# Block 1's up projection from its fifth group on: one product moves the high and low parts of x, and the convolution opens from their sum

## What is computed

```python
h = rmsnorm(x, ffn_norm_g[layer])
up = causal_dwconv(h @ ffn_w_up[layer], ffn_conv_w[layer], ffn_conv_b[layer])   # 1024 -> 5632, then 3 taps along the tokens
gate, val = jnp.split(up, 2, axis=-1)                                            # 2816 each
x = x + (jax.nn.silu(gate) * val) @ ffn_w_down[layer]
```

## Time and profile before

| | us |
|---|---|
| median of 3 runs (lowest, highest) | 1839.29 (1838.99, 1840.1) |
| the profiled execution | 1838.47 |
| its span, first to last instruction | 1836.7 |
| TensorE busy | 1822.3 |
| VectorE busy | 1336.1 |
| ScalarE busy | 1023.9 |

### The profile page before, as it was taken

How to read it: one execution, slowest core, us unless ns; L and a number is a source line. 1 busy time by engine, 2 the same in 40 slices (tenths; PEclk the granted TensorE clock), 3 DMA queues, 4 the chain that set the end, 5 groups by cost and what they waited for, 6 DMA issues and landing times.

```text
span 1836.7 us, 26700 instructions
## 1 busy us (share of the span) xinstructions
PE 1822.3 (99%) x10726; PEld 1601.4 (87%) x10726; DVE 1336.1 (73%) x1898; ACT 1023.9 (56%) x1216; POOL 6.6 (0%) x14
## 2 busy tenths in 40 slices
PE   8999999999999999999999999999999999999998
PEld 7888889998988888899988888898888888889887
DVE  6968887986696887798656555679956555578974
ACT  6557645555565774565445456465544456555543
POOL 0000000000000000000000000000000000000000
PEclk9999999999999999999999999999999999999999
DMA  9976656555887765655555566565556566555553
GB/s 221 195 150 160 184 166 195 193 184 192 165 172 158 166 162 183 202 182 181 184 195 171 170 192 202 161 206 184 184 186 196 160 188 201 172 172 185 191 179 103
DMA packets 253315, 330.15 MB, mean 180 GB/s; under 512 B 25796, under 2 KB 165328, under 8 KB 253192
## 3 DMA queue, kind: packets, MB, share of 16 engines
q1 hardware_dynamic: 252928, 328.10, 61.0%
q10 hardware_dynamic: 264, 0.35, 0.1%
HBM read 327.33 MB, written 1.09 MB: 179 GB/s over the span
## 4 chain that ended last, share of the span: by engine, by line
PE 96%; DVE 2%; DMA 1%; DVEq 1%; SPq 0%; ACT 0%; issue 0%; ACTq 0%
PE psum L618 20%; PE psum L630 16%; PE psum L632 16%; PE psum L631 16%; PE psum L694 12%; PE psum L696 5%; PE psum L721 4%; DMA w_raw<-in_w_in 1%; PE psum L693 1%; DVEq L1471 1%; PE psum L753 1%; DVE xbc L1587 1%; PE psum L842 0%; PE psum L969 0%; PE psum L1006 0%; PE psum L986 0%
## 5 line engine op out<-in xcount | busy, mean ns | idle before, releaser
L419 ACT ACTIVATE w_hi<-w_raw 128x2048 fp32r<-128x2048 f32 (+2 forms) x310 | 575.9, 1858 | 286.1 <-PE psum L632 272.9
L411 DVE TENSOR_TENSOR w_low<-w_raw,w_hi 128x1024 fp32r<-128x1024 f32 (+1 forms) x310 | 372.8, 1203 | 260.6 <-ACT w_hi L419 253.2
L630 PE MATMUL psum<-w_hi,act 128*128 128x512 f32 x1280 | 505.4, 395 | 0.2 <-DVE w_low L411 0.2
L632 PE MATMUL psum<-w_hi,act 128*128 128x512 f32 x1280 | 498.9, 390 | 0.0
L631 PE MATMUL psum<-w_low,act 128*128 128x512 f32 x1280 | 498.4, 389 | 0.0
L618 PE MATMUL psum<-act,w_hi 128*128 128x256 f32 x2112 | 383.3, 284 | 0.3 <-DVE act L1569 0.3
L412 DVE TENSOR_TENSOR w_low<-w_raw,w_hi 128x1024 fp32r<-128x1024 f32 (+2 forms) x310 | 362.9, 1171 | 0.0
L618 PEld LDWEIGHTS psum<-act,w_hi 128*128 128x128 f32 x2112 | 329.3, 192 | 2.9 <-issue 1.4
L694 PE MATMUL psum<-act,w_hi 128*128 128x512 f32 x960 | 330.4, 398 | 0.0
L618 PE MATMUL psum<-act,w_low 128*128 128x256 f32 x1056 | 298.6, 283 | 0.0
L632 PEld LDWEIGHTS psum<-w_hi,act 128*128 128x128 f32 x1280 | 240.2, 188 | 50.9
(11 more groups left out here) (267 smaller groups left out, 1484.9 us busy)
## 6 DMA issues: line engine op xcount, KB each, us to landing
w_raw<-in_w_in SPq DMA_DIRECT2D x123, 1024.0 KB, 5.9
w_raw<-in_ffn_w_up SPq DMA_DIRECT2D x40, 1024.0 KB, 5.1
w_raw<-in_w_up SPq DMA_DIRECT2D x40, 1024.0 KB, 5.1
w_raw<-in_ffn_w_down SPq DMA_DIRECT2D x16, 1024.0 KB, 5.0
w_raw<-in_w_down SPq DMA_DIRECT2D x16, 1024.0 KB, 4.9
w_raw<-in_w_branch_b SPq DMA_DIRECT2D x8, 1024.0 KB, 5.0
w_raw<-in_w_out SPq DMA_DIRECT2D x8, 1024.0 KB, 5.0
w_raw<-in_w_a SPq DMA_DIRECT2D x8, 1024.0 KB, 5.4
```

What stands on the lines that cost most here:

```text
L411: dve.tensor_tensor(lo[:, 0:cut, :], of[:, 0:cut, :], hi[:, 0:cut, :], ALU.subtract).then_inc(w_lo_front, 1)
L419: act.activation(group_view(whi, q % HIGH, g), group_view(raw, q % LOW, g), ACT.Copy).then_inc(w_hi, 1)
L630: mm(o, xh, hi[:, k, :], start=g["opens"] and k == 0, stop=False)
L632: last = mm(o, xl, hi[:, k, :], start=False, stop=g["closes"] > 0 and k == g["kt"] - 1)
```

## The change

In block 1, the groups UP4 to UP21 of both layers get form D in place of form A, and with it two banks each. ScalarE copies the first half of each bank into `up_sum` (`up_halves`: a helper made of lines that block 2 had inline), VectorE adds the second half (`up_whole`, now shared by both blocks), drains and signals `up_whole`. The convolution opens from that sum, and the taps read it. For these groups ScalarE's order at group n becomes: copies; `up_act` (odd n) or `gated_high` (even n); `split_behind`; `up_open`. VectorE's becomes: `up_whole`; `split_behind`; the taps; then `gate_up` or `gated_low`. The order at all other groups stays. The plan gives later groups other banks of the same ring.

```diff
--- before.py
+++ after.py
@@ -92,7 +92,8 @@
         ("BB", 4, (4, 4), 512, const(A_YB), "W", "dve"),
         ("BC", 2, (4,), 512, const(A_YC), "W", "dve"),
         ("OUT", 4, (4, 4), 512, const(A_MG), "W", "dve"),
-        ("UP", 2 * FP, 8, 256, const(A_H2), "A", "dve"),
+        ("UP", UP_WIDE, 8, 256, const(A_H2), "A", "dve"),
+        ("UP", range(UP_WIDE, 2 * FP), 8, 256, const(A_H2), "D", "dve"),
         ("DN", 2 * len(DN_K), DN_K, 512, const(A_G), "W", "dve"),
     ], ring, CHAIN_BANKS)
     plan2 = lambda ring: plan_block([
@@ -383,9 +384,9 @@
             at = 2048 + (g["n"] // 2 % 2) * 1024 + (g["n"] % 2) * 512
             return tmp[:, at:at + 512].rearrange("p (k t) -> p k t", t=S)
 
-        def up_half_count(i, g, t):
-
-            return i * 2 * (2 * FP - UP_WIDE) + 2 * (g["n"] - UP_WIDE) + t + 1
+        def up_half_count(b, i, g, t):
+
+            return layer(b, i) * 2 * (2 * FP - UP_WIDE) + 2 * (g["n"] - UP_WIDE) + t + 1
 
         def by_token(tiles):
 
@@ -1127,10 +1128,20 @@
                     else:
                         A(into(t, g["c0"]), PJ[:, g["banks"][t], :], func, scale=scale[:, t:t + 1]).then_inc(taken["act"], 1)
 
-            def conv_open(b, i, g, wkey, bkey, taps, tap, tiles, dst, done):
+            def up_halves(b, i, n, g):
+
+                for t in range(TT):
+                    if t == 0:
+                        act.wait_ge(step("first_tile"), first_tile_count(at_group(b, i, n)))
+                    else:
+                        arrived(b, i, n)
+                    A(up_sum(g)[:, t, :], PJ[:, g["banks"][t], 0:S], ACT.Copy).then_inc(step("up_half"), 1)
+
+            def conv_open(b, i, g, wkey, bkey, taps, tap, tiles, dst, done, whole=None):
 
                 for t in range(2):
-                    last = A(dst[t], bank(g)[:, t * S:(t + 1) * S], ACT.Identity, bias=col(b, bkey, tiles[t]),
+                    src = bank(g)[:, t * S:(t + 1) * S] if whole is None else whole[:, t, :]
+                    last = A(dst[t], src, ACT.Identity, bias=col(b, bkey, tiles[t]),
                              scale=col(b, wkey, tiles[t] * taps + tap))
                 last.then_inc(step(done), 1)
 
@@ -1272,6 +1283,11 @@
                         if kind in ("V", "GV") or (kind == "QK" and m == 3):
                             act.drain().then_inc(step(dict(QK="qk_in", V="v_in", GV="vg_ready")[kind]), 1)
                         return
+                    if kind == "UP" and g["form"] == "D":
+                        if g["n"] >= 6:
+                            act.wait_ge(step("up_free"), layer(1, i) * FP + g["n"] // 2 - 1)
+                        up_halves(1, i, n, g)
+                        return
                     if g["taker"] == "act" or kind in ("XBC", "UP"):
                         arrived(1, i, n)
                     pair = bank(g).rearrange("p (k t) -> p k t", t=S)
@@ -1294,7 +1310,11 @@
                         act.wait_ge(step("up_free"), layer(b, i) * FP + m - 1)
                     buf = ypair(m % 2, val)
                     t0 = 2 * m + val * FT
-                    conv_open(b, i, g, "fw", "fb", 3, 2 if b == 1 else 1, (t0, t0 + 1), (buf[:, 0, :], buf[:, 1, :]), f"up_open{b}")
+                    whole = None
+                    if g["form"] == "D":
+                        act.wait_ge(step("up_whole"), i * (2 * FP - UP_WIDE) + g["n"] - UP_WIDE + 1)
+                        whole = up_sum(g)
+                    conv_open(b, i, g, "fw", "fb", 3, 2 if b == 1 else 1, (t0, t0 + 1), (buf[:, 0, :], buf[:, 1, :]), f"up_open{b}", whole)
 
                 def up_act(b, i, m, func):
                     act.wait_ge(step("up_conv"), layer(b, i) * FP + m + 1)
@@ -1322,8 +1342,15 @@
                         residual(1, i, g)
                     if MERGED.get(g["name"]) == 1:
                         merged_high(1, i, 1)
+                    if g["kind"] == "UP" and g["form"] == "D":
+                        if g["n"] % 2:
+                            up_act(1, i, g["n"] // 2, ACT.Silu)
+                        else:
+                            gated_high(1, i, g["n"] // 2 - 1)
                     if g["name"] not in FIRST:
                         split_behind(1, i, n)
+                    if g["kind"] == "UP" and g["form"] == "D":
+                        up_open(1, i, g)
                     if g["name"] != "OUT3":
                         residual(1, i, g)
                     if g["name"] == "DN0":
@@ -1331,7 +1358,9 @@
                     if g["name"] in after:
                         after[g["name"]]()
                     if g["kind"] == "UP":
-                        if g["n"] % 2 == 1:
+                        if g["form"] == "D":
+                            pass
+                        elif g["n"] % 2 == 1:
                             up_act(1, i, g["n"] // 2, ACT.Silu)
                         elif g["n"] >= 2:
                             gated_high(1, i, g["n"] // 2 - 1)
@@ -1403,12 +1432,7 @@
                             last = A(ahi[:, A_PO + 2 * m + t, :], pair[:, t, :], ACT.Copy, scale=col(2, "ps", 2 * m + t))
                         last.then_inc(step("po_hi"), 1)
                     elif kind == "UP" and g["form"] == "D":
-                        for t in range(TT):
-                            if t == 0:
-                                act.wait_ge(step("first_tile"), first_tile_count(at_group(2, i, n)))
-                            else:
-                                arrived(2, i, n)
-                            A(up_sum(g)[:, t, :], PJ[:, g["banks"][t], 0:S], ACT.Copy).then_inc(step("up_half"), 1)
+                        up_halves(2, i, n, g)
                     elif kind == "UP" and m % 2 == 0:
                         up_open(2, i, g)
 
@@ -1589,6 +1613,14 @@
                         ordered()
                 return last
 
+            def up_whole(b, i, g):
+
+                for t in range(TT):
+                    dve.wait_ge(step("up_half"), up_half_count(b, i, g, t))
+                    v = up_sum(g)[:, t, :]
+                    TTo(v, PJ[:, g["banks"][t], S:2 * S], v, ALU.add).then_inc(taken["dve"], 1)
+                ordered()
+
             def params_used():
 
                 dve.drain().then_inc(step("layer_done"), 1)
@@ -1918,6 +1950,9 @@
                               yrstd if kind == "BB" else None)
                     elif kind in ("OUT", "DN"):
                         residual(1, i, n, g)
+                    elif kind == "UP" and g["form"] == "D":
+                        up_whole(1, i, g)
+                        dve.drain().then_inc(step("up_whole"), 1)
                     elif kind == "UP":
                         up_take(1, i, n, g)
 
@@ -1950,12 +1985,15 @@
                     t0 = 2 * m + val * FT
                     if b == 1:
                         dve.wait_ge(step("up_open1"), i * (2 * FP) + g["n"] + 1)
-                        last = conv_taps(1, i, g, "fw", 3, ((1, 1), (0, 2)), (t0, t0 + 1), (buf[:, 0, :], buf[:, 1, :]))
-                        last.then_inc(taken["dve"], 1)
+                        wide = g["form"] == "D"
+                        last = conv_taps(1, i, g, "fw", 3, ((1, 1), (0, 2)), (t0, t0 + 1), (buf[:, 0, :], buf[:, 1, :]),
+                                         up_sum(g) if wide else None)
+                        if not wide:
+                            last.then_inc(taken["dve"], 1)
                         if not val:
                             dve.drain().then_inc(step("up_conv"), 1)
                     elif not val and g["form"] == "D":
-                        up_whole(i, g)
+                        up_whole(b, i, g)
                         for t in range(2):
                             V.tensor_scalar(buf[:, t, :], up_sum(g)[:, t, :], col(2, "fw", (t0 + t) * 3 + 1), col(2, "fb", t0 + t), ALU.mult, ALU.add)
                         ordered()
@@ -1967,14 +2005,6 @@
                         last.then_inc(taken["dve"], 1)
                         dve.drain().then_inc(step("up_conv"), 1)
 
-                def up_whole(i, g):
-
-                    for t in range(TT):
-                        dve.wait_ge(step("up_half"), up_half_count(i, g, t))
-                        v = up_sum(g)[:, t, :]
-                        TTo(v, PJ[:, g["banks"][t], S:2 * S], v, ALU.add).then_inc(taken["dve"], 1)
-                    ordered()
-
                 def gate_up(b, i, n, g):
 
                     m = g["n"] // 2
@@ -2027,6 +2057,8 @@
                         early[g["name"]]()
                     if g["name"] not in FIRST and MERGED.get(g["name"]) != 0:
                         split_behind(1, i, n)
+                    if g["kind"] == "UP" and g["form"] == "D":
+                        up_take(1, i, n, g)
                     residual_low(1, i, g)
                     if g["name"] in after:
                         ordered()
```

## The result

| | median us (lowest to highest) | runs |
|---|---|---|
| before | 1839.14 (1838.11 to 1840.1) | 4 |
| changed | 1880.17 (1879.48 to 1880.82) | 4 |

The changed kernel is **slower**: ratio 1.0227, 95% interval 1.0214 to 1.0239. The forecast was 1880.5 us.

What follows compares the result with a forecast made beforehand. TensorE was taken as the bound until the ring of ScalarE and VectorE waits starves it: 20.6 us lost a layer, 41.2 for two, on 1838.47 gives 1879.7, plus 0.8 for the median, 1880.5 us; own range 1876 to 1885.

Steps and rivals of the forecast that it cites:

- The bound and the gain of the product: TensorE bounds the kernel; wider products in UP4 to UP21 save 0.12 us a group, 4.3 us for both layers.
- The Trainium skill's price for a product: Columns / 2.4 + 2.5 ns for each product; by it the gain would be 1.4 us in all.
- The ring: Block 1's wide groups: ScalarE and VectorE each wait twice for the other, 14.02 us per two groups against TensorE's 11.28.
- seven terms: One turn, two groups: 2.55 + 2.27 + 1.90 + 0.69 + 2.51 + 2.27 + 1.83 us, two crossings plus VectorE's work.
- The stock of weights: Weights made three groups ahead delay TensorE's first wait to group 9 at 349.33; DN3 starts at 461.8, not 441.16.
- VectorE's own work: Two groups cost VectorE 11.49 us against TensorE's 11.28; weights made ahead cover the 2 us lost in a layer.
- The second drain: On VectorE behind `up_whole`; taken as 0.09 us, between bounds of 0 and 0.17 us.
- DN0's second tile: It waits for `up_whole(20)` at about 444.8, is done at 447.5 ahead of DN1's weights, and costs nothing more.
- Idle times: In block 1's UP stretch TensorE idles 1.0 and 1.7 us between groups, VectorE about 1 and 1.6 us before line 411.
- One crossing alone: Rival: rounding after `gated_high` is already done, so a turn takes 12.37 us and the kernel 1854 us; chance 0.04.
- The rival of the clock: TensorE's idling in the ring lowers the granted clock, giving 1885 to 2000 us; chance 0.06.

Runs made afterwards that it cites:

- e1: Changed kernel with ScalarE rounding the weights of group n+3 ahead of silu or the gated product's high part in the wide groups; 1835.2 us.
- e8: e1 plus one ScalarE copy of 512 columns ahead of `gated_high` in each even wide group; 1835.01 us.
- e7: e1 with one of the two drains behind `up_whole` taken out for block 1; 1834.26 us, ratio to before 0.9976.
- e2: Changed kernel with the rounding of weights moved ahead of silu in the odd wide groups alone; 1864.77 us.
- e3: Changed kernel with the rounding of weights moved ahead of the gated product's high part in the even wide groups alone; 1850.52 us.
- e5: Changed kernel plus one ScalarE copy of 512 columns ahead of `gated_high` in each even wide group; 1889.81 us.
- e6: Changed kernel with the wide form and its order only in block 1's last eight up groups, UP14 to UP21; 1858.34 us.

## Why the prediction was right

- **The bound and the gain of the product.** 5.64 for 5.76 us a group, 4.3 us in all, was read from block 2. With the ring open it is there: 3.6 us in e1, 3.9 in e8, 4.6 in e7, with intervals of about 1.7 us to either side.
- **The Trainium skill's price for a product** (TensorE: Matmul & The Clock Gate, section Back-to-back issue gap) would have made this 1.4 us, an estimate, and e1 a ratio of 0.9992, which lies outside the intervals of e1 (up to 0.999), e7 and e8, though by little. The section gives that price for an isolated product and says itself that in a stream of products with a weight load each the spacing is another. Here a product of 256 columns took 120 ns (5.76 us for 48) against 109 by that price, and the trace was the better guide.
- **The ring.** 14.02 us a turn by seven terms from rows of before; 14.02 measured. e2, e3 and e5 change it by the amounts of its own terms, e1 opens it. That a waiting instruction holds what is behind it is what e1 shows: the same instructions in another order are 45 us apart. This agrees with the Trainium skill (same page, section Architectural detail: the array is 16× 32×32, not 1× 128×128), which has the queues of ScalarE and VectorE strictly first in, first out.
- **The stock of weights.** First wait at group 9, worked out as 349.6 and measured at 349.42; DN3 461.8 and 461.49, of which 0.2 us is that this execution was 0.2 us ahead when the stretch began (the gating product of pair 1 at 330.93, 331.15). The total is closer than its parts: 20.3 and 21.0 us a layer against 20.6 for each, so the two misses cancel.
- **VectorE's own work.** 11.49 us a turn worked out, 11.49 in e1. The 0.2 us above TensorE's turn are covered, as said, but only just (0.03 and 0.21 us of waiting at DN3 in e1). The second drain was taken at 0.09 us and is 0.045 (e7); what stands ahead of it was read that much too short.
- **DN0's second tile** waited for `up_whole(20)` until 444.08 (worked out: 444.8), and DN1 still had to wait 0.39 us more for its weights, so it cost nothing more, as said. e6 shows that this was near: with a bank of UP21 the wait was 8.06 us.
- **Idle times.** For TensorE I gave 1.0 and 1.7 us; the rows show 0.73 and 1.46. The rows count from the modelled end of the last product, 0.27 us behind its slot; the distances between starts are as worked out. For VectorE I gave about 1 and 1.6 us; its rows show 1.05 and 1.84, drains of 0.18 us included.
- **Rivals.** One crossing alone was priced at 12.37 us a turn and 1854 us; e3, which opens the same crossing by another way, has 12.36 us and 1850.5 us; I had priced eight turns a layer, and nine gain. The rival of the clock did not come in the changed kernel, whose granted clock stays at 1.00 in the stretch, but came for a short time in e5 and e6 (below).

## What to carry to other kernels

When a change puts a wait on another engine ahead of work that this other engine needs, draw the ring: list each engine's order, follow the waits round until you are back, add the start-to-start durations and compare with the period of the bound engine. Busy shares don't show it; in the last section's last row VectorE is idle for 23% of the time and ScalarE for 43%. Weights made three groups ahead hide such a ring for its first turns only, and the repair that worked here, one block of lines moved, is to issue what the bound engine waits for ahead of anything that waits.

## What was not expected of the hardware

The granted clock fell in e5 although TensorE was never idle for more than 2.00 us there (busy 80% of the stretch ahead of it), where the changed kernel with at most 1.6 us (84%) kept 1.00. Busy time by stretch, e5 first, then the changed kernel:

```profile
380.00:395.00 15.00, 12.07 (x65) 10.06 (x66) 11.25 (x20) 8.84 (x15) 0.00 (x0) 1.00 0.45 149
395.00:400.00 5.00, 5.00 (x21) 4.29 (x21) 3.85 (x8) 2.37 (x3) 0.00 (x0) 0.66 0.46 162
```

```profile
349.00:440.00 91.00, 76.83 (x418) 63.58 (x416) 70.33 (x119) 51.69 (x81) 0.00 (x0) 1.00 0.46 151
```

No rule can be read from these rows: from 415 to 450 us of the same execution of e5 TensorE was busy for 27.82 of 35 us (79%), with idle times of 2.00 us again, and the granted clock was 1.00. What made it fall at 395 us stays open.

In e5 it cost nothing that can be measured (9.6 us more, 9.5 worked out without it): TensorE was waiting for weights anyway and used the idle time up. In e6, where it fell behind an idle time of 8.06 us and TensorE was the bound again, 9 products fewer in 8 us are some 2 us. With the 8.06 us and less the 1.0 us that eight wide groups gain, that is 9.1 us a layer, of the 9.7 by which e6 is slower than the kernel before.
